# The loads of a down chunk's seven operands, in the order in which the products use them

## The reference, cut to what matters

```python
c = b_conv + sum(w_conv[i] * a_ext[:, i:i + S] for i in range(CONV_W))
out = (jax.nn.gelu(c) * val) @ w_down      # (S, 2816) @ (2816, 1024)
x = x + out
```

## Time and profile before

| | |
|---|---|
| median of 3 runs | 1659.09 us (1658.59 to 1660.10) |
| profiled execution: time, span | 1657.78 us, 1656.0 us |
| granted clock of TensorE, mean | 0.994 |
| PE busy | 1624.0 us, 98% of the span |
| DVE, ACT busy | 1125.3 us (68%), 696.1 us (42%) |
| DMA over the span | 136 GB/s |

### The profile page before, as it was taken

The page is one execution under the profiler, slowest core; times in us unless marked ns, Lnnn a source line. Parts: engine busy times, 40 slices in busy tenths (PEclk is TensorE's granted clock), DMA queues, the critical chain, the costliest instruction groups (busy, mean ns, idle before and its releaser), DMA issues.

```text
span 1656.0 us, 32499 instructions
## 1 busy us (share of the span) xinstructions
PE 1624.0 (98%) x12958; PEld 1584.1 (96%) x12958; DVE 1125.3 (68%) x2053; ACT 696.1 (42%) x1282; POOL 57.6 (3%) x125
## 2 busy tenths in 40 slices
PE   6999999999999999999999999999999999999998
PEld 6999999999999999999999999999999999999997
DVE  6566565656657869652525888888888776767566
ACT  6344444444444426442434544433333334343312
POOL 2000000000000000000012100000000000000001
PEclk8999999999999999999999999999999999999999
DMA  7444434343437774574443233333333327363122
GB/s 246 152 149 117 133 108 135 100 138 101 128 109 206 235 227 154 198 235 132 139 145 107 59 106 105 106 106 106 106 106 104 128 73 267 119 240 104 68 79 109
DMA packets 272473, 227.03 MB, mean 137 GB/s; under 512 B 43336, under 2 KB 223364, under 8 KB 272324
## 3 DMA queue, kind: packets, MB, share of 16 engines
q1 hardware_dynamic: 141054, 158.81, 28.8%
q10 hardware_dynamic: 131269, 66.15, 14.2%
HBM read 150.56 MB, written 74.36 MB: 136 GB/s over the span
## 4 chain that ended last, share of the span: by engine, by line
PE 75%; DVE 2%; DMA 2%; issue 1%; ACT 1%; DVEq 0%; ACTq 0%; POOL 0%; SPq 0%
PE ps L2294 66%; PE ps L2508 3%; DMA lo_f<-g_spill 1%; PE ps L2545 1%; PE ps L2428 1%; PE ps L2370 1%; DMA raw<-in_w_down_dram 1%; PE ps L2400 1%; PE ps L2418 0%; PE ps L2405 0%; PE ps L2388 0%; PE ps L2527 0%; ACT op_hi L1237 0%; DVE w_lo L1605 0%; DVE op_lo L1644 0%
## 5 line engine op out<-in xcount | busy, mean ns | idle before, releaser
L2294 PE MATMUL ps<-op_hi,w_hi 128*128 128x272 f32 x3696 | 780.5, 292 | 14.1 <-issue 5.1
L2294 PE MATMUL ps<-op_hi,w_lo 128*128 128x272 f32 x3696 | 765.9, 289 | 0.0
L2294 PE MATMUL ps<-op_lo,w_hi 128*128 128x272 f32 x3696 | 763.6, 288 | 0.0
L2294 PEld LDWEIGHTS ps<-op_hi,w_hi 128*128 128x128 f32 x3696 | 580.2, 189 | 30.9 <-issue 29.0
L2294 PEld LDWEIGHTS ps<-op_lo,w_hi 128*128 128x128 f32 x3696 | 581.9, 189 | 0.0
L2294 PEld LDWEIGHTS ps<-op_hi,w_lo 128*128 128x128 f32 x3696 | 578.7, 189 | 0.0
L1605 DVE TENSOR_TENSOR w_lo<-raw,w_hi 128x512 fp32r<-128x512 f32 x256 | 174.4, 699 | 177.3 <-ACT w_hi L1203 177.2
L1203 ACT ACTIVATE w_hi<-raw 128x512 fp32r<-128x512 f32 x256 | 153.9, 625 | 129.8 <-PE ps L2294 90.3
L1282 ACT ACTIVATE u<-ps 128x544 f32<-128x544 f32 x100 | 62.4, 624 | 226.0 <-PE ps L2294 225.9
L1203 ACT ACTIVATE w_hi<-w_f 128x512 fp32r<-128x512 f32 x150 | 90.0, 625 | 34.4 <-DVE w_f L1625 29.0
L1605 DVE TENSOR_TENSOR w_lo<-w_f,w_hi 128x512 fp32r<-128x512 f32 x150 | 99.0, 685 | 3.3 <-ACT w_hi L1203 2.9
(11 more groups left out here) (190 smaller groups left out, 1492.3 us busy)
## 6 DMA issues: line engine op xcount, KB each, us to landing
in_spill<-quad SPq DMA_DIRECT2D x88, 272.0 KB, 2.2
raw<-in_w_up_dram ACTq DMA_DIRECT2D x44, 512.0 KB, 5.0
raw<-in_w_in_dram ACTq DMA_DIRECT2D x42, 512.0 KB, 5.3
g_spill<-value_out SPq DMA_DIRECT2D x22, 544.0 KB, 2.7
t_spill<-t_buf SPq DMA_DIRECT2D x8, 1088.0 KB, 4.5
lo_f<-g_spill SPq DMA_DIRECT2D x8, 1088.0 KB, 8.1
lo_f<-t_spill SPq DMA_DIRECT2D x8, 1088.0 KB, 10.3
raw<-in_w_down_dram ACTq DMA_DIRECT2D x16, 512.0 KB, 5.2
```

What stands on the lines that cost most here:

```text
L2294: last = pe.matmul(out[:, h, 0:HB], (w_hi, w_lo)[a][place][:, j, :], (op_hi, op_lo)[b][at][:, j, HB * h:HB * h + HB], start=fresh and j == ...
```

## The change

The second and third hunk are the tables of ScalarE and of VectorE. The first one is SP's. No instruction is added or removed on any engine.

```diff
@@ SP, background
                 for g in range(5, GENS):
-                    if p == FIRST_PAIR[g] - 1 and j == 0 and 0 < n:
-                        load_chunk(g, (0, 1, 2, 3, 7, 5)[n - 1])
-                    if p == FIRST_PAIR[g] and (n, j) == (0, 1):
-                        load_chunk(g, 6)
-                    if p == FIRST_PAIR[g] and (n, j) == (5, 0):
-                        load_chunk(g, 4)
+
+                    if p == FIRST_PAIR[g] - 1 and j == 0 and n in (1, 2, 5):
+                        load_chunk(g, {1: 0, 2: 1, 5: 7}[n])
+                    if p == FIRST_PAIR[g] and (n, j) in ((0, 1), (1, 0), (2, 0), (3, 0), (5, 0)):
+                        load_chunk(g, {0: 6, 1: 2, 2: 3, 3: 5, 5: 4}[n])
@@ ACT, operands
                     if p == FIRST_PAIR[g] - 1:
-                        todo = {(4, 0): (0,), (5, 2): (1,)}.get((n, j), ())
+                        todo = {(4, 2): (0,), (5, 2): (1,)}.get((n, j), ())
@@ DVE, operands
                     if p == FIRST_PAIR[g] - 1:
-                        lows = {(4, 3): (0,), (6, 1): (1,)}.get((n, j), ())
+                        lows = {(5, 1): (0,), (6, 2): (1,)}.get((n, j), ())
                     if p == FIRST_PAIR[g]:
-                        lows = {(1, 1): (7,), (2, 1): (6,), (3, 1): (2,), (4, 1): (3,), (5, 3): (5,)}.get((n, j), ())
+                        lows = {(0, 3): (7,), (2, 1): (6,), (3, 1): (2,), (4, 1): (3,), (5, 1): (5,)}.get((n, j), ())
```

## The result

The changed kernel takes 1664.74 us (median of 7 runs, 1662.61 to 1665.63), the one before 1659.09 (7 runs): 1.0036 of before, 95% interval 1.0026 to 1.0046. It is 5.7 us slower, where the prediction had 1658.8 and a range up to 1662.0.

What follows compares the result with a forecast made beforehand. PE, busy 98% of the span, bounds the kernel, so only its holes can be won. Removed 9.23 us and added 8.92 give net -0.3: median 1658.8 us, range 1654.5 to 1662.

Steps and rivals of the forecast that it cites:

- What moves in fact: On ACT nothing changes order; on DVE only op_lo of operand 0 goes behind Q22's combine; otherwise only SP's loads move.
- Holes a and c: PE waits before the last products of pairs 55 and 59, 1.67 and 1.90 us; forecast to shrink by 1.67 and 1.83.
- T: Time at which PE starts a chunk's first pair (56 or 60); forecast 1381.0 and 1475.8 after the change.
- Operand 5: Last of SP's loads, landing at T + 17.8 (17.05 to 18.5), leaving 3.7 us holes before pairs 57 and 61.
- By the trace the weights are in time: With work in both queues, ACT's weights go ahead of SP's operand loads (1011 packets to 88), so they land in time.
- The third rival: Weights of a chunk's second pair land last, T + 17.3; DVE waits at L1616; hole 4.7 us, 1662.3 us; chance 0.14.
- The clock: PE's lower clock after the new holes before pairs 57 and 61 costs 0.76 us per chunk, bounds 0 and 1.52.
- The sum: Over both chunks: removed 9.23 us, added 2 x (3.7 + 0.76) = 8.92, net -0.3 us, median 1658.8.

Runs made afterwards that it cites:

- the turn: Kernel before with one edit: on DVE the low part of operand 0 goes behind Q22's adds and combine, SP's loads unchanged; 1.0007 of before.
- weights on SP: Changed kernel, with the weights of pairs 57 and 61 issued from SP's queue behind operand 6 instead of ACT's; 1662.86 us, 1.0028 of the kernel before.

## Why the prediction was wrong, point by point

- *What moves in fact.* Right. Over 1350 to 1520 ACT's instructions, by name, stand in the same order in both kernels, and DVE's differ only in the two low parts of operand 0. One low part and SP's loads carry all of it.
- *Holes a and c close.* Right, to 0.1 us. That they were won, 3.5 us, was right only as all else counted from T; with the old loads the turn won nothing.
- *Operand 5.* Right in size, at the early bound, and in part by luck: forecast T + 17.8, bounds 17.05 to 18.5. In the changed kernel T is 1382.2 and its load landed at 1399.24, T + 17.0, and 10.0 us behind it would have been a hole of 2.9 us. It was not what ended last. The sum has all of the weights' bytes ahead of it, which was not so here; where they were (weights on SP) it landed at T + 18.1 and, in chunk 6, T + 18.8.
- *"By the trace the weights are in time".* This is the step that failed. I read 1011 packets against 88 in the earlier trace rows as a priority of ACT's queue. It was the end of SP's queue: operand 6's load was the only thing left in it. Its semaphore rises in sixteen steps as its parts land, from 1391.77 to 1394.75, and eight of them had come by 1392.21. The counts run out the same way: 73 of SP to 424 of ACT over 1392 to 1393, and over 1393 to 1394:

```profile
q10 hardware_dynamic: 587, 0.30, 108.8%
q1 hardware_dynamic: 15, 0.03, 6.8%
```

The profile doesn't say on which DMA engine a packet ran, but this fits an end on some of the engines first, where ACT's packets then had no rival. With four loads in SP's queue the counts are equal, and the weights landed at T + 18.1 and T + 18.5, after operand 5. The third rival happened: its mechanism, its place (L1616) and its point (after T + 16.2) were all on paper, with a chance of 0.14; its landing (T + 17.3) and its hole (4.7, where 5.49 and 5.91 were measured) were too low. The rule of the Trainium skill that the prediction names (DMA: Bandwidth & Descriptors, Queues, rings and completion order) and this window spoke against each other, and I let the window decide without asking whether both queues were full in it.

- *The clock.* 0.76 us per chunk was taken as half of 1.52; 2.35 and 2.16 were measured, above both bounds, 0 and 1.52: a loss seen once was no upper bound.
- *The sum.* By the third rival with the measured hole and clock: 5.49 + 5.91 + 2.35 + 2.16 - 9.23 = +6.7 on the profiled run. The medians say +5.7.

With the weights in time on SP's queue 1662.86 was measured (1.0028), not 1658.8 either. Two terms are larger there: a hole of 4.3 to 4.7 for 3.7 and a clock of 2.3 to 2.7 for 0.76. As that run also has operand 5 land 1.1 us later than in the changed kernel, it does not tell what the changed kernel would have taken with its weights in time and all else as it was; that stays open.

## What to carry to other kernels

Loading operands in the order in which they are used is no gain where the first part of the list can be fetched early: here the loads of 2 and 3 had been issued 13 and 10 us before T, and holding them back packed 4.5 MB into the time in which a queue on another engine had to bring its own 1 MB. What counts is what is in flight when the next thing with a date is issued. Put transfers whose order matters on one queue; in two queues the one with the small packets loses while the other is full (0.31 MB to 1.26 here). Such a move has a price too: what stands behind on that queue waits along (SP's 2.7 us for the last low weights). And before a shared window is read for who has priority, find one in which both sides have work to the end.

## What the runs showed of the hardware

- Two queues with work: 597 to 597, 436 to 440, 582 to 580 packets, of 2176 and of 512 bytes. In the first window that is 1.26 to 0.31 MB.
- At the end of one queue's work the counts look like a priority of the other: 73 to 424, then 15 to 587 packets per microsecond in the kernel before.
- The lower clock behind a hole: none behind 2.13 us, 1.6 us lost behind 2.28, 1.5 behind 2.66, 1.5 behind 3.93, and 2.2 to 2.7 behind 3.72, 4.26, 4.50, 4.68, 5.49, 5.69 and 5.91, all in this stage. The step from no loss to a loss of 1.6 us lay between two holes that differ by 0.15 us. A hole of 3.72 cost more than one of 3.93, and one of 5.84 cost 1.5, as the granted clock had gone to 0.50 inside it, over 3 us before PE went on (0.67 over 1509 to 1510, 0.50 from there, PE on at 1512.94). So the length alone doesn't fix the price.
